# Delta-rule inversion on one block parity, and head norms moved behind the memory keys

## The reference, cut to what matters

```python
lower = where(strict, beta[t] * kk * decay, 0)          # strictly lower triangular
sol   = triangular_solve(lower + eye, rhs)              # rhs = [v*beta, k*beta*exp(g)]
v_new = u - w @ S ;  o = q_dec @ S + attn @ v_new       # scan over chunks, per head
o = rmsnorm(o, head_gain) * silu(gate)                  # per head
x = x + o @ w_out
x = x + mem_cross_attn(rmsnorm(x), memn, wq, wk, wv, wo)   # keys and values come from memn alone
```

## Time and profile before

| | |
|---|---|
| median of 3 runs | 1736.66 us |
| profiled execution | 1722.62 us, of which the span is 1720.8 us |
| PE / PEld busy | 1603.2 us (93%) / 1514.6 us (88%) |
| ACT, DVE, POOL busy | 808.1, 796.1, 1188.0 us |
| chain that ended last | PE 52% of the span, DVE 7%, ACT 1% |
| delta rule, from DVE's first preparation step to the first key product | 592.55 to 725.09 us |
| memory keys and values | 725.09 to 770.40 us |

### The profile page before, as it was taken

How to read it: one execution, slowest core, us unless ns; L and a number is a source line. 1 busy time by engine, 2 the same in 40 slices (tenths; PEclk the granted TensorE clock), 3 DMA queues, 4 the chain that set the end, 5 groups by cost and what they waited for, 6 DMA issues and landing times.

```text
span 1720.8 us, 32818 instructions
## 1 busy us (share of the span) xinstructions
PE 1603.2 (93%) x12776; PEld 1514.6 (88%) x12776; DVE 796.1 (46%) x1430; ACT 808.1 (47%) x1169; POOL 1188.0 (69%) x920
## 2 busy tenths in 40 slices
PE   4979999999999987999999996989999999899997
PEld 3976998999988785999999995978999999799997
DVE  6038366320166465636532004655655335575523
ACT  3473544554455435444455442555555443644442
POOL 3733994899967600098589993653899988279995
PEclk7998999999999998999999998999999999999999
DMA  5421553565544300055355552432566654155552
GB/s 213 160 88 63 172 181 111 172 196 192 191 157 154 116 1 1 13 173 181 110 173 191 193 195 72 136 111 84 175 196 195 193 168 143 58 169 193 195 196 98
DMA packets 67086, 248.55 MB, mean 144 GB/s; under 512 B 7440, under 2 KB 7696, under 8 KB 66448
## 3 DMA queue, kind: packets, MB, share of 16 engines
q1 hardware_dynamic: 66960, 246.69, 43.8%
HBM read 245.62 MB, written 1.05 MB: 143 GB/s over the span
## 4 chain that ended last, share of the span: by engine, by line
PE 52%; DVE 7%; ACT 1%; issue 1%; DVEq 0%; ACTq 0%
PE ps_dve L361 42%; PE ps_act L361 10%; DVE x_lo L1378 1%; DVE x_hi L1375 1%; PE ps_act L372 1%; DVE xT L1370 1%; DVE work L1711 1%; ACT work L977 1%; DVE work L1409 0%; DVE sq L1363 0%; DVE work L1705 0%; ACT work L931 0%; DVE sq L1343 0%; DVE xT L1328 0%; DVE x_lo L1335 0%
## 5 line engine op out<-in xcount | busy, mean ns | idle before, releaser
L326 POOL TENSOR_TENSOR ring_lo<-ring,ring_hi 128x512 fp32r<-128x512 f32 x916 | 1187.8, 1335 | 511.5 <-ACT ring_hi L917 508.5
L917 ACT ACTIVATE ring_hi<-ring 128x1024 fp32r<-128x1024 f32 x458 | 465.8, 1052 | 193.3 <-DMA ring<-panels 190.9
L361 PE MATMUL ps_dve<-x_hi,ring_hi 128*128 128x256 f32 x1728 | 415.6, 281 | 17.6 <-DVE x_lo L1378 17.4
L361 PE MATMUL ps_dve<-x_lo,ring_hi 128*128 128x256 f32 x1728 | 412.9, 279 | 0.0
L361 PEld LDWEIGHTS ps_dve<-x_hi,ring_hi 128*128 128x128 f32 x1728 | 328.8, 190 | 23.2 <-DVE x_lo L1378 18.9
L361 PEld LDWEIGHTS ps_dve<-x_lo,ring_hi 128*128 128x128 f32 x1728 | 329.1, 190 | 0.2
L361 PE MATMUL ps_dve<-x_hi,ring_lo 128*128 128x256 f32 x1728 | 243.1, 278 | 0.0
L361 PE MATMUL ps_dve<-work_parts,ring_hi 128*128 128x256 f32 x1728 | 225.3, 276 | 0.0
L361 PEld LDWEIGHTS ps_dve<-x_hi,ring_lo 128*128 128x128 f32 x1728 | 219.1, 190 | 0.2 <-POOL ring_lo L326 0.2
L361 PEld LDWEIGHTS ps_dve<-work_parts,ring_hi 128*128 128x128 f32 x1728 | 211.8, 188 | 0.0
L1370 DVE TENSOR_TENSOR xT<-xT,ps_dve 128x512 f32<-128x512 f32 x40 | 27.5, 688 | 325.7 <-PE ps_dve L361 325.1
(11 more groups left out here) (232 smaller groups left out, 2199.0 us busy)
## 6 DMA issues: line engine op xcount, KB each, us to landing
ring<-panels SPq DMA_DIRECT2D x458, 512.0 KB, 3.4
consts<-constants SPq DMA_DIRECT2D x1, 2208.0 KB, 14.8
xT<-x_t SPq DMA_DIRECT2D x1, 1024.0 KB, 5.0
memn<-mem_t SPq DMA_DIRECT2D x1, 1024.0 KB, 18.9
out_t<-xT SPq DMA_DIRECT2D x1, 1024.0 KB, 3.9
smalls<-small_operands SPq DMA_DIRECT2D x1, 849.5 KB, 7.9
consts<-constants SPq DMA_DIRECT2D x1, 129.5 KB, 4.8
angle_i<-positions SPq DMA_DIRECT2D x1, 128.0 KB, 6.3
```

The costliest lines, as they stand in the source:

```text
L326: pool.tensor_tensor(ring_lo[:, s, cs], ring[:, s, cs], plain(ring_hi[:, s, cs]), ALU.subtract).then_inc(sem("lo_made"), 1)
L361: ins = pe.matmul(o, lhsT, rhs, start=start, stop=stop, skip_group_check=True)
L917: tell(act.activation(ring_hi[:, n % RING, :], ring[:, n % RING, :], ACT.Copy), "hi_made")
```

## The change: what it does

- In the levels k = 1 to 6, y is made only for the even blocks of columns of t (`even`), the product for t is made only for the even blocks of columns and the one for tt only for the odd ones (`odd`). Each matmul then has 64 moving columns where it had 128; the stationary side stays 128x128. `dense` is the packed view of a bank with these 4 x 64 columns.
- ACT copies the 256 columns of a group's y into the even columns of `gd_y`, and writes zeros over the odd ones by a second instruction.
- DVE's subtractions are on 256 columns. DVE waits for `y_ready`, and cuts the next level's `gd_b` ahead of both subtractions; PE waits for the renewed t by `t_ready` before it makes y.
- The Silu of the gates (one instruction of 2048 columns before the levels of half 0) becomes four of 512 columns behind levels 1 to 4 of half 0, and one preload of the log/exp table stands behind the levels of each half.
- The norm sums, `rsqrt` and `mix_heads` of both halves move behind: PE makes the sums after the second and third bank of the memory keys (`delta_norms`), ACT does the four `rsqrt` among the key copies, DVE does `mix_heads(0)` and `mix_heads(1)` after `mem_parts`. The squares of all 8 heads are kept (`sq[:, h]`).

```diff
--- before.py
+++ after.py
@@ -239,6 +239,16 @@
         gate = area(6144, 8, T)
         gd_at, gd_t, gd_tt, gd_attn, gd_b, gd_y, gd_vb, gd_kd = (area(8192 + 1024 * i, HALF * 2, P) for i in range(8))
         gd_cols = area(16384, 8, 8)
+
+        def even(m, k):
+            return m.rearrange("p j (a two w) -> p (j a) two w", two=2, w=1 << k)[:, :, 0, :]
+
+        def odd(m, k):
+            return m.rearrange("p j (a two w) -> p (j a) two w", two=2, w=1 << k)[:, :, 1, :]
+
+        def dense(o, k):
+            return o[:, 0:2 * P].rearrange("p (a w) -> p a w", w=1 << k)
+
         gd_row = lambda i: mixT[0:GD_H, (4 + i) % C, :]
         qk_sq = [area(8192 + 512 * i, 2, T) for i in range(GD_H)]
         conv_y = [sq[:, 2 * i:2 * i + 2, :] for i in range(4)]
@@ -749,9 +759,11 @@
                                 flip(o[:, j * P:(j + 1) * P], gd_b[:, 4 * g + j, :], "dve" if j == 3 else None)
                             t_at[g] = told.seen["t_ready"]
                         else:
+                            pe.wait_ge(sem("t_ready"), t_at[g] - (k > 1))
                             o = bank("act", "y_ready")
                             for j in range(4):
-                                mm(o[:, j * P:(j + 1) * P], gd_b[:, 4 * g + j, :], gd_t[:, 4 * g + j, :], True, True,
+                                js = slice(4 * g + j, 4 * g + j + 1)
+                                mm(o[:, j * 64:(j + 1) * 64], gd_b[:, 4 * g + j, :], even(gd_t[:, js, :], k), True, True,
                                    "act" if j == 3 else None)
                             y_at[g] = told.seen["y_ready"]
                     for g in range(2 if k else 0):
@@ -760,11 +772,13 @@
                         if k < LEVELS - 1:
                             o = bank("dve", "t_ready")
                             for j in range(4):
-                                mm(o[:, j * P:(j + 1) * P], gd_tt[:, 4 * g + j, :], gd_y[:, 4 * g + j, :], True, True,
-                                   "dve" if j == 3 else None)
+                                js = slice(4 * g + j, 4 * g + j + 1)
+                                mm(o[:, j * 64:(j + 1) * 64], gd_tt[:, 4 * g + j, :], even(gd_y[:, js, :], k), True,
+                                   True, "dve" if j == 3 else None)
                         o = bank("dve", "t_ready")
                         for j in range(4):
-                            mm(o[:, j * P:(j + 1) * P], gd_y[:, 4 * g + j, :], gd_tt[:, 4 * g + j, :], True, True,
+                            js = slice(4 * g + j, 4 * g + j + 1)
+                            mm(o[:, j * 64:(j + 1) * 64], gd_y[:, 4 * g + j, :], odd(gd_tt[:, js, :], k), True, True,
                                "dve" if j == 3 else None)
                         t_at[g] = told.seen["t_ready"]
                 pe.wait_ge(sem("t_ready"), told.seen["t_ready"])
@@ -793,11 +807,13 @@
                     mm(o[:, 0:P], gd_y[:, 2 * hh, :], gd_attn[:, 2 * hh, :], True, True)
                     mm(o[:, P:2 * P], gd_b[:, 2 * hh + 1, :], gd_attn[:, 2 * hh + 1, :], True, False)
                     mm(o[:, P:2 * P], gd_b[:, 2 * hh, :], qkv4[:, 0, h, P:2 * P], False, True, "act")
-                for g in range(2):
-                    pe.wait_ge(sem("osq"), told.seen["osq"] - 2 + 2 * g)
-                    mm(bank("act", "norm_used"), ones, sq[:, 4 + 2 * g:6 + 2 * g, :], True, True, "act")
-                if half:
-                    memory_side()
+
+            def delta_norms(i):
+                for g in {1: (0, 1), 2: (2, 3)}.get(i, ()):
+                    pe.wait_ge(sem("osq"), osq_at + 2 * g + 2)
+                    mm(bank("act", "norm_used"), ones, sq[:, 2 * g:2 * g + 2, :], True, True, "act")
+            osq_at = told.seen["osq"] - GD_H
+            memory_side(delta_norms)
             out_project()
             xa()
             mlp(1)
@@ -1176,13 +1192,15 @@
                                 (gd_vb[:, 2 * hh + 1, :], gd_cols[:, 3, h:h + 1]))):
                             ins = act.activation(dst, o[:, j * P:(j + 1) * P], ACT.Copy, scale=scale)
                         tell(ins, "act_out")
-                if half == 0:
-                    settle()
-                    tell(act.activation(gate, gate, ACT.Silu), "gate_silu")
-                    log_exp()
                 for k in range(1, LEVELS):
                     for g in range(2):
-                        copy_out(gd_y[:, 4 * g:4 * g + 4, :], name="y_ready")
+                        y = gd_y[:, 4 * g:4 * g + 4, :]
+                        act.activation(even(y, k), dense(take(), k), ACT.Copy)
+                        tell(act.activation(odd(y, k), dense(const("ones"), k), ACT.Copy, scale=0.0), "y_ready")
+                    if half == 0 and k <= 4:
+                        gs = gate[:, 2 * k - 2:2 * k, :]
+                        tell(act.activation(gs, gs, ACT.Silu), "gate_silu")
+                log_exp()
                 for hh in range(HALF):
                     o = take()
                     act.activation(gd_y[:, 2 * hh, :], o[:, 0:P], ACT.Copy)
@@ -1194,12 +1212,15 @@
                     h = half * HALF + hh
                     o = take()
                     act.activation(qkv4[:, 2, h, :], o[:, 0:T], ACT.Copy)
-                    tell(act.activation(sq[:, 4 + hh, :], o[:, 0:T], ACT.Square), "osq")
-                if half:
-                    told.more("mixed", 2)
-                for g in range(2):
-                    rsqrt(2 * T, 1.0 / P)
-            memory_side(1, 0, 4)
+                    tell(act.activation(sq[:, h, :], o[:, 0:T], ACT.Square), "osq")
+            memory_side(1, 0, 2)
+            for g in range(4):
+                if g == 2:
+                    memory_side(1, 2, 3)
+                if g >= 2:
+                    told.more("mixed")
+                rsqrt(2 * T, 1.0 / P)
+            memory_side(1, 3, 4)
             squares("c_out", C, 4)
             xa(1)
             mlp(1)
@@ -1678,9 +1699,6 @@
 
             for half in range(2):
                 for s in range(HALF + 1):
-                    if half and s == 2:
-                        told.more("gate_silu")
-                        mix_heads(0)
                     if s < HALF:
                         h = half * HALF + s
                         o = take()
@@ -1705,10 +1723,8 @@
                     tell(dve.tensor_tensor(gd_b[:, 4 * g:4 * g + 4, :], gd_at[:, 4 * g:4 * g + 4, :],
                                       spread(levels[:, k, :], 4), ALU.mult), "b_ready")
 
-                def renew(m, g):
-                    o = take().rearrange("p (j b) -> p j b", b=P)
-                    m = m[:, 4 * g:4 * g + 4, :]
-                    tell(dve.tensor_tensor(m, m, o, ALU.subtract), "t_ready")
+                def renew(m, k):
+                    tell(dve.tensor_tensor(m, m, dense(take(), k), ALU.subtract), "t_ready")
 
                 for g in range(2):
                     cut(0, g)
@@ -1721,11 +1737,14 @@
                     cut(1, g)
                 for k in range(1, LEVELS):
                     for g in range(2):
+                        told.more("y_ready")
                         if k < LEVELS - 1:
-                            renew(gd_t, g)
                             cut(k + 1, g)
-                        renew(gd_tt, g)
+                            renew(even(gd_t[:, 4 * g:4 * g + 4, :], k), k)
+                        renew(odd(gd_tt[:, 4 * g:4 * g + 4, :], k), k)
             mem_parts()
+            told.more("gate_silu", 4)
+            mix_heads(0)
             mix_heads(1)
             mix_parts([0, 0, 0, 0])
             residual(xa_gain[:, C:2 * C], add=4)
```

## The result

The changed kernel takes **1788.01 us** (median of 4 runs, 1773.93 to 1792.48) where the kernel before took 1743.31 on the same chip (1736.13 to 1753.41, 4 runs): ratio **1.0264**, 95% interval [1.0218, 1.0311]. It is slower by 2.6%, where 0.7% less was forecast. The nearest rival is the one to which the prediction gave 0.04, the clock that stays low in the levels; it stood 32 us above the kernel before (1769 against 1736.66), and 45 us were measured. Each ratio in this text leaves out the executions more than 1.5% above the fastest of their kernel; that is 7 of 10 in e4_filler, 4 of 12 in e9_wide_filler and one of 10 in e3_level1_wide.

The account below looks back on a forecast made before the run. PE's program plus the places where PE waits was taken to bound the kernel. The terms -6.4 - 10.5 - 1.6 + 3.2 + 3.1 gave -12.2 us, from 1736.66 to 1724.5 us, range 1712 to 1735.

Parts of the forecast that it names:

- the clock that stays low in the levels: Rival: clock stays low under 64-column products, a level takes 10.3 us instead of 5.33, time 1769 us; chance 0.04.
- the pace of a record in the narrow levels: Levels: a 64-column PE record takes 0.107 us, set by its weight load, 4% less than a 128-column record.
- nothing is booked for the clock: Both halves' levels: PE still starts them at the low clock as half 0 did before, so no cost was counted.
- Level 1 at the low clock: Level 1, both halves: -1.0 us, bounds 0.6 and 6.0; records stay at 0.21 us if the weight load slows.
- Levels, -6.4 us: Levels 1 to 6, both halves: -3.8 us for levels 2 to 5, -1.6 for level 6, -1.0 for level 1.
- Short runs at nothing: Runs of 2, 4 and 8 floats made by `even` and `odd` in SBUF were costed at nothing.
- Preparation of half 1, -10.5: Before half 1's levels: -8.4 us without `mix_heads(0)` and the `rsqrt` wait, -2.1 without norm sums; bounds 9 and 11.5.
- Tail: Keys and values behind the levels: -1.6 us norm sums gone, +3.2 four sums among the keys, +3.1 PE waiting.
- the one wait of 3.1 us for low parts: First values: PE waits 3.1 us for panel 9's low part, delayed by ACT's `rsqrt`; bounds 1.2 and 6.7.
- The sum: Whole kernel: all terms together -12.2 us, from 1736.66 to 1724.5 us, -0.7%.

Follow-up runs that it names:

- e4_filler: Changed kernel, all levels narrow, plus four unread 512-column products in each half's idle times ahead of level 1: 1747.27 us, ratio 1.0055.
- e9_wide_filler: Changed kernel with the levels back at 128 columns, plus four unread 512-column products ahead of level 1 in each half: 1721.38 us, ratio 0.9881.
- e3_level1_wide: Changed kernel with level 1 alone back at 128 columns, levels 2 to 6 at 64: 1724.77 us, ratio 0.9943.
- e10: Changed kernel with level 1 at 128 columns and each 64-column product of levels 2 to 6 issued twice: 1780.68 us, ratio 1.026.
- e1_wide: Changed kernel with products, copies and subtractions of the levels back at 128 columns, new wait order and moved norms kept: 1722.67 us, ratio 0.9943.
- e11_y_wide: Changed kernel with only y (8 of a level's 24 products) and its copy back at 128 columns: 1740.42 us, one run.
- e5: Changed kernel with the levels' moving operands read as 64 adjacent columns, so the inverse is not the right one: 1768.22 us, one run.
- e8: Changed kernel with levels at 128 columns, some ACT panel casts made earlier, and four unread 512-column products in each half: 1727.11 us, ratio 0.9947.

## Why the prediction was wrong

**The step that failed** is the pace of a record in the narrow levels, 0.107 us, and with it the sentence that nothing is booked for the clock. It was taken from the earlier trace rows, narrow products at a clock of 1.00. Those rows show that narrow products keep a high clock for 3.60 us, and e10 shows it over 50 us. But the levels begin at the low clock, and what had to be shown is that it rises under narrow products. No row of before shows that: in level 1 of both halves it was 128-column products that did. The prediction said of them that their pace is the weight load's "or nearly", and took that for the same load on the array; e1_wide, e3_level1_wide and e11_y_wide against the changed kernel show that it is not. What the runs show in its place: 0.213 us a record at a granted clock of 0.50 through all six levels of both halves.

The rival that named this had the right price for a level, 10.3 us forecast and 10.24 measured, but not the whole: it gave 32 us more than the kernel before, and 45 were measured. It kept level 1 at 7.9 us, which took 10.70 (5.7 us over both halves); level 6 took 7.6 us where its 45 us imply 7.0 (1.3); it had nothing for the solves, which also begin at the low clock (3.7), nor for the preparation of half 0 (3.2, not of the change); the preparation of half 1 took 1.3 of this back. Its chance of 0.04 rested on an argument that the runs refute: that the clock had risen under records of the same pace.

The Trainium skill (TensorE: Matmul & The Clock Gate, section Part 1: The HAM clock gate) says that the clock depends on how busy the array has been, and that activity releases the throttle. If "busy" is read as the profile's busy time, the changed kernel contradicts it: PE and PEld were busy 41.02 of 41.02 us at 0.50. The measurement decides: an engine that is busy in the profile's sense can stay at the low level for a whole stage.

The other steps:
- *Level 1 at the low clock*: the bound that a record stays at 0.21 us because the load slows with the clock was right, 0.213 with 64 columns and with a third of the records at 128 (e11). But the 7.9 us for level 1 took over from the kernel before that the clock rises halfway, and it did not.
- *Levels, -6.4 us*: the record was 0.113, not 0.107, at the high clock, so the narrow part of the gain is nothing: e3_level1_wide and e1_wide have equal ratios (0.9943), 5.52 and 5.47 us a level. No run explains why the 65-column records of the earlier trace rows are at 0.107. What did help is the new order, 0.33 us a level in e1_wide.
- *Short runs at nothing*: right, 10.24 us a level with and without them (e5), 5.52 with them at the high clock (e3).
- *Preparation of half 1, -10.5*: measured -11.8, just outside its bounds of 9 to 11.5. The forecast let half 1 take the 15.20 us that half 0 takes from DVE's first step; it took 13.87 (686.67 to 700.54). Half 0's 15.20 had a mean clock of 0.85 in it, and half 1 now had 0.99; the 1.3 us between them go with that clock, for which nothing was booked.
- *Tail*: -1.6 + 3.2 + 3.1 = +4.7 forecast, +4.4 measured (47.21 to 51.65). The sum is near by some luck: the one wait of 3.1 us for low parts did not come. The changed kernel's PE timeline has five waits of 2.45 us together instead, 0.53 for the bank of the sums, 0.48 for a cast and three for low parts (0.47, then 0.62 at 805.37 and 0.35 at 811.64); and the four norm sums took 0.9 us each, not 0.8:

```profile
790.09 0.38 PE L371 MATMUL ps_act<-x_hi,ring_hi 128*128 128x256 f32 x1 [0.53 <-DVE rstd L1336]
796.30 0.36 PE L371 MATMUL ps_act<-ring_hi,x_hi 128*128 128x256 f32 x1 [0.48 <-ACT ring_hi L933]
798.83 1.21 PE L371 MATMUL ps_act<-ring_lo,x_hi 128*128 128x256 f32 x8 [0.47 <-POOL ring_lo L336]
```

- *The sum*: with the clock mended, e1_wide's stretch is 10.5 us shorter than before (178.16 to 167.65) and e1_wide 0.57% faster, 9.9 us. The forecast of -12.2 was near that of a kernel whose levels raise the clock.

**Left open**: why the clock rises under 128-column products and not under 64, and where it falls in the long executions of e4_filler. The same spare products ahead of wide levels gave no execution with such a low mean clock in the 22 runs of e8 and e9 (0.964 to 0.974). Nor is the number of columns the whole of it. In the preparation of half 0 of the changed kernel the clock fell at about 598, with PE busy without a gap, and stayed at 0.50 for 10 us, under products of 256 columns and of 512 (the latter with 8 rows only) among others; in the kernel before it fell at the same place and was back at 1.00 within 4 us (593 to 597). Five of these 10 us:

```profile
600.00:605.00 5.00, 5.00 (x11) 2.70 (x12) 2.46 (x7) 2.79 (x11) 0.00 (x0) 0.50 0.31 107
```

## What to carry to other kernels

Before narrowing a product, ask two things of the profile: whether its record already has the length of its weight load (then fewer columns gain nothing), and at which granted clock the stretch begins. A row with the new shape at a high clock shows only that the shape keeps the clock; look for one in which it rises. Where a stretch starts at the low clock, a few wide products first, in a place where PE waits anyway, can be worth more than the columns saved: here 3.5 us in the stages ahead of wide levels, while ahead of narrow ones the same products gave times from 1716 to 1777 us. A high clock at the start of a narrow stretch is thus not enough in every execution.

## What the runs showed that was not expected

- The granted clock has memory: identical 64-column products ran for 50 us at 1.00 behind a wide level (e10, 0.112 us a record) and for 59 us at 0.50 without it (0.213).
- PE and PEld were busy 41.02 of 41.02 us and the granted clock was still 0.50. A busy PE did not hold a high clock in the preparation either (600 to 605, 0.50). With y at 128 columns and nothing else changed it rose to 1.00, in level 1 of one half and in level 2 of the other (e11).
- At the low clock a record of 64 columns and one of 128 take the same 0.21 us, and at the high clock the same 0.11. The weight loads keep the pace of the records at both: 32 of them start from 630.74 to 637.57 in the changed kernel, 0.213 each, so the load slows with the clock.
